# Filler products of TensorE at stage boundaries, and two modulation sums moved within their stages

## The reference, cut to what matters

```python
mod_l = (silu_c @ mod_w[i] + mod_b[i]).reshape(B, 1, N_MOD, D_MODEL)
mod_c = (silu_cc @ mod_w[i] + mod_b[i]).reshape(1, N_MOD, D_MODEL)
sh1, sc1, gt1, sh2, sc2, gt2 = [mod_l[:, :, s] for s in range(N_MOD)]
u_l = rmsnorm(lat, norm_g[i, 0]) * (1 + sc1) + sh1
y_c, y_l = mlstm_mixer(u_c, u_l, ...)            # layer 0; layer 1: hgrn2_mixer
lat = lat + gt1 * rmsnorm(y_l, norm_g[i, 1])
u_l = rmsnorm(lat, norm_g[i, 2]) * (1 + sc2) + sh2
lat = lat + gt2 * rmsnorm(ffn(u_l), norm_g[i, 3])  # layer 0: swiglu; layer 1: moe_swiglu
```

## Time and profile before

| | us |
|---|---|
| median of 3 runs | 2103.58 |
| lowest, highest | 2100.83, 2109.34 |
| profiled execution | 2115.88 |
| its span, first to last instruction | 2114.2 |
| TensorE busy | 1896.8 |
| VectorE busy | 1428.8 |
| ScalarE busy | 1001.4 |
| GpSimd busy | 113.2 |

### The profile page before, as it was taken

One profiled execution on the slowest core, in us unless ns is written; L12 is line 12 of the kernel. 1 busy time (PEld: TensorE's weight loads), 2 busy tenths in 40 slices (PEclk: granted clock), 3 DMA queues, 4 the chain that ended last, 5 costly groups with the idle time before them and its releaser, 6 DMA issues. The chain is left out here.

```text
span 2114.2 us, 25835 instructions
## 1 busy us (share of the span) xinstructions
PE 1896.8 (90%) x9774; PEld 1614.1 (76%) x9774; DVE 1428.8 (68%) x1543; ACT 1001.4 (47%) x1125; POOL 113.2 (5%) x120
## 2 busy tenths in 40 slices
PE   7999986869999996899966759999999999999996
PEld 2677665658778885788856649898989898989895
DVE  2575365455454556576449448889898988888887
ACT  3323222342222223422344236777777767676765
POOL 1000011000000000000039000000000000000000
PEclk9999586989999998799987869999999999999998
DMA  7354110223433453344410029999999999999994
GB/s 252 111 191 156 31 40 1 80 91 130 168 122 127 156 179 114 100 150 140 160 40 1 0 88 332 319 354 318 338 333 336 338 332 334 328 345 328 340 331 167
DMA packets 245886, 412.27 MB, mean 195 GB/s; under 512 B 7689, under 2 KB 161457, under 8 KB 245691
## 3 DMA queue, kind: packets, MB, share of 16 engines
q1 hardware_dynamic: 244470, 411.25, 56.9%
q10 hardware_dynamic: 1350, 0.11, 0.0%
HBM read 410.29 MB, written 1.05 MB: 195 GB/s over the span
## 5 line engine op out<-in xcount | busy, mean ns | idle before, releaser
L2160 DVE TENSOR_TENSOR w_low<-e_ring,w_high 128x1408 fp32r<-128x1408 f32 (+2 forms) x384 | 617.4, 1622 | 103.6 <-ACT w_high L2097 100.8
L2097 ACT ACTIVATE w_high<-e_ring 128x1408 fp32r<-128x1408 f32 (+2 forms) x384 | 528.6, 1382 | 215.7 <-PE ps L2010 213.2
L2008 PE MATMUL ps<-w_high,list_h 128*128 128x352 f32 x1024 | 338.2, 330 | 18.0 <-DVE w_low L2160 16.4
L2010 PE MATMUL ps<-w_high,list_l 128*128 128x352 f32 x1024 | 329.8, 322 | 0.0
L2009 PE MATMUL ps<-w_low,list_h 128*128 128x352 f32 x1024 | 329.2, 322 | 0.0
L2008 PEld LDWEIGHTS ps<-w_high,list_h 128*128 128x128 f32 x1024 | 192.9, 188 | 26.7 <-DVE w_low L2160 25.8
L1305 ACT ACTIVATE fw_high<-ring 128x1024 fp32r<-128x1024 f32 x66 | 70.0, 1060 | 278.1 <-PE ps L1254 188.0
L1339 DVE TENSOR_TENSOR fw_low<-ring,fw_high 128x1024 fp32r<-128x1024 f32 x66 | 80.9, 1225 | 174.8 <-ACT fw_high L1305 174.8
L2009 PEld LDWEIGHTS ps<-w_low,list_h 128*128 128x128 f32 x1024 | 193.8, 189 | 0.3
L2010 PEld LDWEIGHTS ps<-w_high,list_l 128*128 128x128 f32 x1024 | 192.7, 188 | 0.0
L1252 PE MATMUL ps<-u_high,fw_high 128*128 128x512 f32 x352 | 140.3, 399 | 6.9 <-DVE fw_low L1339 6.9
(11 more groups left out here) (344 smaller groups left out, 3476.9 us busy)
## 6 DMA issues: line engine op xcount, KB each, us to landing
e_ring<-in_e_w_gu_dram SPq DMA_DIRECT2D x128, 1408.0 KB, 8.0
e_ring<-in_e_w_down_dram SPq DMA_DIRECT2D x32, 1536.0 KB, 7.3
bg_area<-in_mod_w_dram SPq DMA_DIRECT2D x80, 512.0 KB, 4.0
e_ring<-in_e_w_down_dram SPq DMA_DIRECT2D x32, 1280.0 KB, 7.6
ring<-in_f_w_gu_dram SPq DMA_DIRECT2D x22, 1024.0 KB, 7.1
ring<-in_h_w_in_dram SPq DMA_DIRECT2D x10, 2048.0 KB, 7.9
ring<-in_m_w_in_dram SPq DMA_DIRECT2D x6, 2048.0 KB, 7.9
ring<-in_f_w_down_dram SPq DMA_DIRECT2D x5, 2048.0 KB, 7.9
```

The lines of the kernel that those rows point to most:

```text
L2008: nc.tensor.matmul(out, high[:, f, :], w_high[:, c, :], start=(f == 0), stop=False)
L2010: last = nc.tensor.matmul(out, low[:, f, :], w_high[:, c, :], start=False, stop=(f == total - 1))
L2097: nc.scalar.activation(piece(k.w_high, p), raw(p), ACT.Copy).then_inc(S.high_done, 1)
L2160: nc.vector.tensor_tensor(piece(k.w_low, p), raw(p), piece(k.w_high, p).bitcast(F32), ALU.subtract).then_inc(S.low_done, 1)
```

## The change

A helper issues `count` products of the identity with a column of ones spread to 256 columns, into a PSUM bank whose content nobody needs at that point; nothing reads the result. It is called at the end of mlstm_in (6), at the start of mlstm_heads (4), at the start of mixer_out (14 for four tiles, 8 for two), behind the sum of "mo" (8), at the end of mixer_out (20 and 10), at the start of each norm_in (10, 10 and 6), at the start of feed_forward (6) and at its end (18), and in hgrn_in behind the first sum (6). Vector 1's sum stands behind values(0), its take behind turn 2, and vector 2's accumulation starts at turn 2 and ends behind the last turn. In "mo", take(2) stands in the loop over heads, behind head 3, and scale behind the loop.

```diff
+def keep_active(k, bank, count):
+
+    for _ in range(count):
+        k.nc.tensor.matmul(k.ps[:, bank, 0:256], k.ident[:, :], k.ones[:, 0:1].to_broadcast([P, 256]), start=True, stop=True)
...
@@ norm_in, tensor @@
+            keep_active(k, 0, 2 * len(tiles) + 2)
             for n, i in enumerate(tiles):
...
@@ mlstm_in, tensor, at the end @@
+            keep_active(k, 6, 6)
...
@@ mlstm_heads, tensor @@
+            keep_active(k, 7, 4)
             scores(0)
             spread_m(0)
             spread_m(1)
-            k.bg.sum(pe, 1, 0, 7, 0)
             for n in range(turns):
...
                 if n:
                     values(n - 1)
+                if n == 1:
+                    k.bg.sum(pe, 1, 0, 7, 0)
             values(turns - 1)
...
@@ mlstm_heads, vector @@
                 if n:
                     finish(n - 1)
-                else:
+                if n == 2:
                     k.bg.take(dve, 1, 0, 7)
-                k.bg.op(dve, 16 + n // 2, n % 2)
+                if n >= 2:
+                    k.bg.op(dve, 16 + (n - 2) // 2, n % 2)
             finish(turns - 1)
+            k.bg.item(dve, 23)
...
@@ mixer_out, vector @@
-            if last_mod is not None:
-                k.bg.take(dve, last_mod, 0, 0)
-                k.bg.scale(dve, last_mod)
...
                 if h in split_behind:
                     w.split_low(dve, split_behind.index(h))
+                if h == 3 and last_mod is not None:
+                    k.bg.take(dve, last_mod, 0, 0)
+            if last_mod is not None:
+                k.bg.scale(dve, last_mod)
             low(HEADS - 1)
...
@@ mixer_out, tensor @@
+            keep_active(k, 0, 3 * n_t + 2)
             if last_mod is not None:
                 k.bg.sum(pe, last_mod, 0, 0, 0)
+                keep_active(k, 1, 8)
             pe.wait_ge(normed, n_t)
...
+            pe.wait_ge(r.copied_a, 1)
+            keep_active(k, t0, 5 * n_t)
...
@@ feed_forward, tensor @@
+            keep_active(k, 5, 6)
             for g, c in enumerate(chunks):
                 group(g, c)
+            pe.wait_ge(y_added, 8 * (last_g + 1) + 2)
+            keep_active(k, 0, 18)
...
@@ hgrn_in, tensor @@
             bg.sum(pe, 7, 0, 7, 0)
+            keep_active(k, 0, 6)
```

## The result

The changed kernel took 2120.0 us in the median (five runs, 2116.8 to 2120.8) against 2103.6 us of the kernel before (2100.8 to 2109.3): a ratio of 1.0071, interval 1.0055 to 1.0088. That is slower by 16 us, where 2102.7 and a range up to 2114 had been forecast. In a second comparison, both on one chip, it was 2117.6 us (12 runs, 2112.7 to 2119.6) against 2109.3 us (35 runs, 2101.0 to 2119.3), ratio 1.0039, interval 1.0022 to 1.0056. The two intervals barely touch; both say slower, by 8 to 16 us. The kernel before itself spreads over 18 us, the changed one over 7.

A forecast was written before the change was run, and what follows sets the result against it. The matmul engine was taken as the bound in the long stages, losing time at 0.50 after idle boundaries. Terms -1.0 + 1.1 + 3.4 - 3.3 - 1.5 + 2.6 - 2.2 = -0.9 us, against the 2103.6 median: 2102.7 us, range 2089 to 2114.

The forecast's parts named there:

- "mo": Start of mixer_out: turns 0.8 us earlier behind fillers, first piece +4.2 us from the later take; together +3.4 us.
- the same sum: Whole kernel: the terms' -0.9 us, set against the 2103.6 us median as well as the profiled 2115.9 us, giving 2102.7.
- The heads' term: Start of mlstm_heads: fillers warm scores and spreads, moving the sum frees nothing; -1.0 us, cases from -5.1 to +5.2.
- the second rival: Clock does not rise within mo's 22 fillers, turns begin 25.9 us into the stage; 2112 us; chance 0.13.
- End of the heads: End of mlstm_heads: two accumulation steps of vector 2 stand behind the last turn; +1.1 us (0 to +2.5).
- n1 and feed_forward: norm_in n1 and start of feed_forward: fillers put transposes and first products at 1.00; -3.3 us (-4.0; +3 if cold).
- n2 and hgrn_in: norm_in n2: faster transposes, -1.5 us (-2.5 to +3); hgrn_in: fillers delay the first piece, +2.6 (to +5.2).
- ho, n3, routing: Mixer_out "ho", norm_in n3 and router: turns -0.3, transposes -1.1, router -0.8; together -2.2 us (-3.1 to 0).
- The first (heads hold 1.00): Rival: mlstm_heads holds 1.00 from its warm start; 12.6 us below the forecast, 2090; chance 0.17.
- The third: Rival: the fillers do not lift the clock at all, so no term is a gain; about 2135 us; chance 0.06.
- The fourth: Rival: clock falls within the transposes despite fillers; gains of n1, n2 and n3 stay away; 2107 us; chance 0.04.
- what was to show the prediction wrong: Mean clock over 0.85 in mlstm_heads, mo's first piece under 24 us in, or a span change over 10 us.

The follow-up runs named there:

- gap-filled kernel: The changed kernel with five more fillers between the second spread and values(0), ahead of the loop over the turns: 2112.4 us.

## Why the prediction was wrong

The heads of all traces, from the start of scores(0) to the end of the last values, say most of it:

| us | sum ahead of the pairs | sum behind values(0) |
|---|---|---|
| no fillers ahead | 125.5, 111.0, 113.9 | 118.6, 122.3 |
| fillers ahead | 109.1, 105.8, 109.2, 108.6, 105.7, 108.7 | 119.2, 119.7, 115.5, 119.7 |

(The stage begins 1.9 us later with the fillers, 5.6 us after the last product of mlstm_in instead of 3.7. The gap-filled kernel, 113.6, is not in the table.)

**Where the sum was set: the step that failed.** The terms gave -0.9 us against the profiled execution, and between the two profiled executions the span changed by +0.9. That the two lie so near is luck: the heads took 6.3 us less than in that long execution and the stages from hgrn_state to routing 4.4 less, by a jump that comes without fillers too, while "mo", the end of the heads and hgrn_in took more than forecast. But then I set "the same sum" against the median, reading the 12 us between them as luck in the heads. The reading was right in the main (125.5 and 111.0 us in two traces of one kernel), the step was not: it holds only if the change leaves the good executions good. With the sum moved and the gap open, six traces of five kernels have heads of 115.5 to 122.3 us and none is near 111. Against the trace of before that stands near its median (2107.2 us) the heads went from 3.7 + 111.0 to 5.6 + 119.2, +10 us, outside my -5.1 to +5.2.

**The heads' term.** "The move itself frees nothing: the engine must do the sum before scores(1) either way" put the price of the move at nothing and left out what the sum covered: the wait for the mask. The term was -1.0 us; from the end of mlstm_in to the end of the heads it measured +10 against the trace of before near its median, 1.9 of it the later start. I had that wait in the sum as a start of values(0) at 223.4 and still counted the move as free, because I weighed each product at either level and not what follows when the engine stops. The run with only the sum moved shows +7 us without any filler, and the sum put back takes 9.8 off. That the clock would fall before the sum ended was forecast, and came; that it would stay at 0.50 for 30.7 us was not.

**"mo".** The mechanism was right, and one term was too small. The turns came 18.7 us in (forecast 16.6): the first 14 fillers (28 records) took 8.5 us, as forecast (8.6), the sum 4.2 instead of 3.6, and the last 8 fillers 6.5 instead of 4.4, since the clock was at 0.50 again from 352.5 to 359.3. Then the take: 10.4 us from turns to piece, as forecast. Together +5.6 instead of +3.4, 29.2 us in; leaving out the fillers gave 5.6, moving the take 4.7. The condition of the second rival, "whatever the matmul engine does longer is lost" from 11.5 us on, is what happened, though the clock did rise within the fillers and the turns began 7 us earlier than that rival had them. The first gated copy began 19.4 us in, not 16 to 18. I named the price of fillers ahead of work that DVE has ready, and did not ask what a take behind the normalising would give: a first piece 6.2 us earlier than in the kernel before (17.4 us in, not 23.6).

**End of the heads.** +2.0 instead of +1.1, in all eight traces with the late products (5.05 us of idle PE instead of 3.02): the two accumulation steps took 3.47 us instead of the 2.48 of the earlier trace rows with POOL's add beside them, and that add 2.23 instead of 1.26.

**n1 and feed_forward.** Right in sign and size. From the last piece of "mo" to the end of feed_forward the traces without these fillers have 411.4, 416.4, 412.8, 411.5 and 416.2 us, those with them 408.5 to 414.2, most near 410. Both rows hold the falls of the clock in the middle of feed_forward, one or two in every trace and 3 to 14 us at 0.50 in all, with and without fillers; with half of that time taken off, the traces without these fillers have 409.4 to 411.3 us and those with them 406.2 to 408.2. So -3, forecast -3.3. n1's transposes took 3.71 us at 1.00 instead of 5.31, and the copies began 3.0 us after the first of them. Not as forecast: the clock fell once more to 0.50 ahead of feed_forward and the fillers there, not the first pieces, paid for the way back (3.2 us at 0.51 above). The Trainium skill ("TensorE: Matmul & The Clock Gate", Part 4: PE-mode transpose) would have had the transposes below full clock; they ran at 1.00.

**n2 and hgrn_in.** From the end of feed_forward to hgrn_in's last piece: 236.5 to 237.4 us in the traces without the fillers there, 236.3 to 240.2 with them, about +1; forecast +1.1 (-1.5 and +2.6). The first piece came 8.3 us after the sum's start instead of 3.4 (+4.9, within the bound of 5.2), and the pieces ran 2.5 us shorter in seven of the eight traces, a gain I had not counted. The exception is the first trace of the changed kernel.

**ho, n3, routing.** Forecast -2.2; n3's transposes took 2.07 us instead of 3.60, but they began 0.7 us later, and from hgrn_in's last piece to the first of the experts a gain of some 0.6 us is left (189.6 to 190.2 us against 190.3 to 190.8 in most traces), beside jumps of 4 us that appear with and without fillers (185.9 and 186.8).

**Slips in the sums.** Three quarters of n3's 1.7 us are 1.3, not 1.1; n2's term comes to -1.4 and not -1.5; values(0) and the sum at 1.00 end at 229.2, not 229.4. Together they move the forecast by 0.1 us.

**The rivals.** The first (heads hold 1.00) did not come in this kernel. With the sum ahead of the pairs the heads take 105.7 to 109.2 us, as short as that rival had them or shorter, though they don't hold 1.00: the clock fell behind scores(0) and again, for some 3 us at a time, in later pairs. The third fell: scores(0) and n1's transposes ran at 1.00 behind fillers. The fourth fell with the transposes. Of what was to show the prediction wrong, none came (a clock of 0.80 in the heads, 29.2 us in "mo", 0.9 us of span), and it was wrong all the same: the first two look for a kernel faster than forecast only, and the third was measured against one execution of before.

## What to carry to other kernels

An execution far from the median of its kernel is no base for a sum: find the stages that make the difference, take a second trace, and ask what the edit does to the good executions. Work that fills a wait is part of the schedule even if nobody waits for its result, so before moving it say what the engine does in its place. Fillers are free only until the inputs of the next real product are ready (11.2 us into "mo", where they held the engine until 18.7). Here a take belonged behind the work that was ready earlier (the normalising) and ahead of the work that wasn't (the gates), not at either end.

## What the runs showed of the hardware

The granted clock of the same instructions in the same order differs between executions: the kernel before ran its heads in 111.0 and 125.5 us, and with fillers ahead and the sum in its place six traces of six kernels lay between 105.7 and 109.2. The clock also fell while the engine was busy without a pause: once or twice in the middle of feed_forward in every trace, and 6.2 us after scores(0) began with the sum right behind the spreads. A sum of 32 records with one column took 6.96 us at 0.50 and 3.63 at 1.00. DVE and POOL were both slower when both added from SBUF at once: 3.47 us for two accumulation steps of DVE instead of 2.48, 2.23 us for POOL's add instead of 1.26. The Trainium skill ("GPSIMD Engine Reference", section 1, Specifications) says that GpSimd shares its SBUF interfaces with VectorE, with contention where a DVE instruction has two SBUF inputs; these rows agree.
